# A decoder layer on one core: the first norm's weights spread by a product with ones, and the first block's units begin with the rounded part

## The reference

```
xn   = x * rsqrt(mean(x*x) + 1e-6) * norm_attn      # per row; norm_attn has 1024 values
proj = xn @ w_in                                    # w_in is 1024 x 6664
```

## Time and profile before

| | |
|---|---|
| median of 3 runs | 1675.35 us (1675.06 to 1676.15) |
| the profiled execution | 1674.95 us, its span 1673.2 us |
| TensorE busy | 1649.5 us, 99% of the span |
| VectorE, ScalarE, POOL busy | 951.2, 633.0, 354.0 us |
| granted TensorE clock, mean | 0.997 of full speed |

### The profile page before, as it was taken

One profiled execution on the slowest core, in us unless ns is written; L12 is line 12 of the kernel. 1 busy time (PEld: TensorE's weight loads), 2 busy tenths in 40 slices (PEclk: granted clock), 3 DMA queues, 4 the chain that ended last, 5 costly groups with the idle time before them and its releaser, 6 DMA issues.

```text
span 1673.2 us, 26883 instructions
## 1 busy us (share of the span) xinstructions
PE 1649.5 (99%) x10087; PEld 1494.9 (89%) x10087; DVE 951.2 (57%) x1745; ACT 633.0 (38%) x1403; POOL 354.0 (21%) x353
## 2 busy tenths in 40 slices
PE   8999999999999999999999999999999999999997
PEld 8999999899998899888978899999999999999995
DVE  5413333443145545674544877777777777766787
ACT  5423334232235423553402444333444443344332
POOL 3002001010002200121000233333333222223354
PEclk9999999999999999999999999999999999999999
DMA  7104354562311132311231111111111111110112
GB/s 218 52 28 134 62 74 86 61 88 30 68 29 26 33 77 45 61 26 26 63 132 51 32 45 51 50 50 50 50 29 46 50 50 50 50 46 30 50 63 107
DMA packets 138714, 99.21 MB, mean 59 GB/s; under 512 B 82360, under 2 KB 128448, under 8 KB 138632
## 3 DMA queue, kind: packets, MB, share of 16 engines
q1 hardware_dynamic: 138632, 98.08, 24.2%
HBM read 88.43 MB, written 11.60 MB: 60 GB/s over the span
## 4 chain that ended last, share of the span: by engine, by line
PE 96%; DVE 2%; issue 1%; DMA 1%; ACT 1%; POOL 0%; SPq 0%; DVEq 0%; POOLq 0%; ACTq 0%
PE bank L887 37%; PE bank L1235 23%; PE bank L1215 6%; PE bank L1268 6%; PE bank L1269 6%; PE bank L1267 6%; PE bank L843 3%; PE bank L1276 2%; PE bank L1072 2%; PE bank L1042 1%; PE bank L952 1%; PE bank L944 1%; PE bank L947 1%; PE bank L989 1%; PE bank L927 0%
## 5 line engine op out<-in xcount | busy, mean ns | idle before, releaser
L1235 PE MATMUL bank<-xT_hi,w_hi 128*128 128x384 f32 (+1 forms) x768 | 250.7, 326 | 1.0 <-DVE xT_lo L1819 1.0
L1235 PE MATMUL bank<-xT_hi,w_lo 128*128 128x384 f32 (+1 forms) x768 | 250.6, 326 | 0.0
L1235 PE MATMUL bank<-xT_lo,w_hi 128*128 128x384 f32 (+1 forms) x768 | 250.5, 326 | 0.0
L887 PE MATMUL bank<-xT_hi,w_hi 128*128 128x384 f32 (+1 forms) x1008 | 195.4, 335 | 0.0
L887 PE MATMUL bank<-xT_hi,w_lo 128*128 128x384 f32 (+1 forms) x1008 | 186.3, 326 | 0.0
L887 PE MATMUL bank<-xT_lo,w_hi 128*128 128x384 f32 (+1 forms) x1008 | 186.1, 326 | 0.0
L2495 POOL TENSOR_TENSOR e<-gain_b,e 128x512 f32<-128x512 f32 x60 | 78.0, 1301 | 435.2 <-ACT gain_b L1748 435.2
L887 PEld LDWEIGHTS bank<-xT_lo,w_hi 128*128 128x128 f32 x1008 | 168.7, 188 | 0.0
L887 PEld LDWEIGHTS bank<-xT_hi,w_lo 128*128 128x128 f32 x1008 | 168.7, 188 | 0.0
L887 PEld LDWEIGHTS bank<-xT_hi,w_hi 128*128 128x128 f32 x1008 | 166.1, 188 | 2.7 <-issue 1.0
L1794 DVE TENSOR_TENSOR w_lo<-raw,w_hi 128x1024 fp32r<-128x1024 f32 (+1 forms) x54 | 70.4, 1303 | 158.6 <-ACT w_hi L1387 158.4
(11 more groups left out here) (261 smaller groups left out, 3025.5 us busy)
## 6 DMA issues: line engine op xcount, KB each, us to landing
raw<-in_w_in SPq DMA_DIRECT2D x64, 256.0 KB, 4.6
raw<-in_w_up SPq DMA_DIRECT2D x16, 1024.0 KB, 5.4
raw<-in_w_down SPq DMA_DIRECT2D x16, 1024.0 KB, 5.0
raw<-in_w_in SPq DMA_DIRECT2D x9, 1024.0 KB, 6.3
xin<-in_x_prompt SPq DMA_DIRECT2D x8, 512.0 KB, 4.0
bc<-gate_rows SPq DMA_DIRECT2D x32, 128.0 KB, 7.2
Cin<-in_state_C SPq DMA_DIRECT2D x4, 1024.0 KB, 7.6
out<-Cin SPq DMA_DIRECT2D x16, 256.0 KB, 9.4
```

The lines of the kernel that those rows point to most:

```text
L887: last = nc.tensor.matmul(out, lhsT, rhs, start=(step == 0), stop=(step == 3 * KT - 1))
L1235: last = nc.tensor.matmul(bank[unit_bank(g, u)][:, 0:cn], w[:, 0, k * WCOLS + tile * P:k * WCOLS + (tile + 1) * P], x[:, k, c0:c0 + cn], s ...
```

## The change

`norm_attn` is no longer loaded 128 times over. It comes as one row of 1024 values (4 KB) into the second buffer of `xn`, as the first transfer of all, ahead of x tile 0. POOL writes a row of 128 ones into the first buffer of `xn`. TensorE multiplies ones and row (inner dimension 1) into banks 0 and 1, 512 columns each, and ScalarE copies both banks into `gain_b` before it squares tile 0. VectorE waits for these copies instead of for the load.

The identity products, 14 in one run before, become 6 ahead of the row's products, 6 behind them and 5 behind the transposes of tile 0.

The units of block 0 wait for the rounded halves of their x tile (`norm_hi`) at their start, and for the remainders (`norm_lo`) only ahead of the second pass, which is the first that reads them.

```diff
--- before.py
+++ after.py
@@ -101,7 +101,7 @@
 B_MLP = len(BLOCKS)
 RING = 3
 SPLIT_AT = 3
-WARM = 14
+WARM = 6
 NB = SEQ // P
 MASKW = WIN + (2 * NSEQ - 1) * DSEQ
 UP_UNITS = 2 * len(CHUNKS)
@@ -403,6 +403,8 @@
         w_hi_half = sem("w_hi_half")
         w_lo_done = sem("w_lo_done")
         gain_in = sem("gain_in")
+        gain_mm = sem("gain_mm")
+        gain_cp = sem("gain_cp")
         const_in = sem("const_in")
         consts = sem("consts")
         norm_sq = sem("norm_sq")
@@ -511,6 +513,8 @@
         out_dma = sem("out_dma")
 
 
+        one_row, gain_row = xn[0:1, 0, 0:P], xn[0:1, 1, :]
+
         def w_view(t, b, k):
 
             n = WCOLS + 8 if b == 0 else WCOLS
@@ -633,8 +637,8 @@
                     sp.wait_ge(norm_xn, i - 2)
                 sp.dma_start(xin[0:rows_of(i), i % 3, :], x_rows(i)).then_inc(x_in[i % 3], 16)
 
+            sp.dma_start(gain_row, norm_attn[0].unsqueeze(0)).then_inc(gain_in, 16)
             load_x(0)
-            sp.dma_start(gain_b[:, :], norm_attn[0].partition_broadcast(P)).then_inc(gain_in, 16)
             load_block(0)
             load_x(2)
             small(bias_i[:, :], b_gate[0, 0:MH].unsqueeze(1))
@@ -869,6 +873,8 @@
                     pe.wait_ge(w_hi_done, b + 1)
                 for step in range(3 * KT):
                     (w, x), k = PASSES[step // KT], step % KT
+                    if b == 0 and step == KT:
+                        pe.wait_ge(norm_lo, 2 * (u + 1))
                     if n == 0 and step == KT // 2:
                         pe.wait_ge(w_hi_done, 1)
                     if n == 0 and step == 2 * KT:
@@ -1179,11 +1185,20 @@
                     proj_unit(b, u)
 
             pe.wait_ge(consts, 1)
-            for x in range(WARM):
-                nc.tensor.matmul(bank[3][:, 0:P], ident[:, :], ident[:, :], start=True, stop=True)
+            def identity_products(n):
+                for x in range(n):
+                    nc.tensor.matmul(bank[3][:, 0:P], ident[:, :], ident[:, :], start=True, stop=True)
+
+            identity_products(WARM)
+            pe.wait_ge(gain_in, 16)
+            for h in range(2):
+                nc.tensor.matmul(bank[h][:, :], one_row, gain_row[:, h * 512:(h + 1) * 512],
+                                 start=True, stop=True).then_inc(gain_mm, 1)
+            identity_products(6)
             norm_transposes(0, xn)
+            identity_products(5)
             for u in range(NT):
-                pe.wait_ge(norm_lo, 2 * (u + 1))
+                pe.wait_ge(norm_hi, 2 * (u + 1))
                 proj_unit(0, u)
                 if u + 2 < NT:
                     norm_transposes(u + 2, xn)
@@ -1642,6 +1657,9 @@
                 act.wait_ge(x_in[i % 3], 16 * (i // 3 + 1))
                 square(i, xin[0:rows_of(i), i % 3, :], junk)
 
+            for h in range(2):
+                act.wait_ge(gain_mm, h + 1)
+                nc.scalar.activation(gain_b[:, h * 512:(h + 1) * 512], bank[h][:, :], ACT.Copy).then_inc(gain_cp, 1)
             square_x(0)
             act.wait_ge(raw_first, 32)
             nc.scalar.activation(w_hi[:, 0, part_cols(0, 0)], raw[:, 0, part_cols(0, 0)], ACT.Copy).then_inc(w_first, 1)
@@ -2106,7 +2124,7 @@
                     nc.vector.scalar_tensor_tensor(h, a, 0.5, h, ALU.mult, ALU.add).then_inc(sg_use, 1)
 
 
-            dve.wait_ge(gain_in, 16)
+            dve.wait_ge(gain_cp, 2)
             norm_tile(0, xin[:, 0, :], xn)
             dve.wait_ge(w_first, 1)
             at = part_cols(0, 0)
@@ -2371,6 +2389,7 @@
                                                channel_multiplier=ch)
 
             nc.gpsimd.memset(neghalf[:, :], -0.5)
+            nc.gpsimd.memset(one_row, 1.0)
             link(nc.gpsimd.memset(ident[:, :], 0.0))
             keep_where(ident[:, :], [[-1, P]], 0, 1, ALU.not_equal, 1.0).then_inc(consts, 1)
```

## The result

The changed kernel takes 1679.03 us (median of 14 runs, 1676.52 to 1679.55), the kernel before, on the same chips, 1675.28 us (14 runs). The ratio is 1.0018, its 95% interval 1.0012 to 1.0025: **slower**, by 3.75 us by the medians and by 2.0 to 4.2 us by the interval. I had forecast 1.5, and the time lies outside my range. The ratio is still just inside the 0.2% that I had called "within"; the medians, 0.22% apart, are not. Twelve of the fourteen runs lie between 1678.96 and 1679.55 us; the other two are 1676.52 and 1677.29.

What follows compares the result with a forecast made beforehand. TensorE, busy 99% of the span, was taken as the bound, so only its start could move: second unit at 19.5 instead of 18.05, +1.5 us with POOL's memset, giving 1676.8 us; range 1675.4 to 1678.1.

Steps and rivals of the forecast that it cites:

- within: Whole kernel: time changes by no more than about 0.2% (3.35 us); chance 0.95.
- part 1 and 2: At the start: gain as a row delays tile 0's square to 6.85 us; norms then put the second unit at 19.5.
- The path: Start: row products and copies delay the first square, then xn of tile 2, moving the second unit from 18.05 to 19.5.
- the price of the row's products: TensorE before the first norm: four fp32 instructions of 512 columns, 0.45 us apart at most, the last 0.59 long.
- at the same place as before: TensorE's start: clock falls only behind tile 0's transposes, which with the first rounding run 10.39 to 12.1 us.
- clock falls in the pause: Rival: TensorE idles 7.5 to 10.4 us, transposes of tile 0 run 0.21 apart; +2.35, 1677.7 us; chance 0.12.
- Held steps: Before xn of tile 2: VectorE's remainder holds POOL's first step until 16.6 us; the second takes 0.55, done at 17.2.
- late row: Rival: row lands 4.9 us after issue, row products start at 5.7 us; +2.85, 1678.2 us; chance 0.06.
- The weights of the first half block: Load at the start: weights land about 1.3 us earlier, near 7.0, but nothing waits for them alone any more.
- Part 3: First block's units begin with the rounded part: first unit waits for roundings at 12.1 us; later units gain nothing.
- The five late identity products: TensorE behind tile 0's transposes: start at 11.26, end near 13.4 us; no cost while xn of tile 2 is later.

Runs made afterwards that it cites:

- experiment 9: The changed kernel run again unaltered: 1678.23 us, second unit at 20.32 us.
- Experiment 3: The changed kernel without the row: gain loaded 128 times over again, no row products or copies; 1674.77 us, second unit at 17.75 us.
- experiment 5: The changed kernel with the square of x tile 0 moved ahead of the two gain copies on ScalarE: 1675.62 us against 1675.54 for the kernel before.
- experiment 4: The changed kernel with 14 instead of 6 identity products ahead of the row's products: 1680.57 us, second unit at 22.78 us.
- experiment 1: The kernel before, with only the first block's units beginning with the rounded part: 1675.16 us against 1675.38, ratio 0.9997.
- 8: The changed kernel without the row, with all 14 identity products ahead of the transposes and five behind: 1675.22 us against 1675.54 for the kernel before.
- experiment 11: The changed kernel without the row, gain loaded 128 times over, measured again: 1674.71 us against 1675.14 for the kernel before, ratio 0.9997.
- experiment 6: The changed kernel without the five identity products behind the transposes of tile 0: 1678.80 us, second unit at 22.87 us.
- 7: The changed kernel with twelve instead of six identity products behind the row's products: 1678.68 us, second unit at 21.93 us.
- 10: The changed kernel run unaltered for a second further look: 1678.96 us, second unit at 22.10 us.
- experiment 2: The changed kernel with row products over 128 rows, the tile zeroed first by VectorE and x tile 0 issued before the row: 1678.04 us, ratio 1.0014.
- experiment 12: The changed kernel with row products over 128 rows and the square of x tile 0 ahead of the gain copies: 1675.19 us against 1675.14, ratio 1.0003.

## Why the prediction was wrong

The steps of part 1 and 2, as forecast, in the first profile and in experiment 9 (start in us):

| step | before | forecast | after | exp. 9 |
|---|---|---|---|---|
| second gain copy | | 6.35 | 8.41 | 6.62 |
| square of tile 0 | 4.76 | 6.85 | 8.91 | 7.11 |
| xn of tile 0 | 6.94 | 9.05 | 11.08 | 9.29 |
| transposes of tile 0 | 8.28 | 10.39 | 12.42 | 10.63 |
| square of tile 1 | 10.25 | 12.0 | 14.92 | 13.13 |
| square of tile 2 | 12.53 | 14.0 | 16.93 | 15.14 |
| xn of tile 2 | 15.52 | 17.25 | 19.91 | 18.12 |
| unit 1 | 18.05 | 19.5 | 22.10 | 20.32 |

**The path was right**: the row's products and copies stand ahead of the first square, the chain of norms runs late, xn of tile 2 holds unit 1, and in the first profile the shift reaches the end one to one. Experiment 3 shows that the row is the cause, experiment 5 that ScalarE's order is part of it.

**The term that failed is the price of the row's products**: "so 0.45 apart at most". The fold's row is right for the upper level, and experiments 4 and 9 measured 1.98 us for the four; but I had read the upper level into the start of this kernel, and added only "a little for the slow clock". At the lower level the four took 3.78 us (0.85 apart, 1.02 for the first). Of the 2.06 us by which the square of tile 0 is later than forecast, about 1.4 are the spacing, 0.5 the longer last product and 0.2 to 0.3 the start of the row's products at 4.60 instead of 4.33: POOL's memset of the ones pushed the identity products from 1.61 to 1.74, where I had said some hundredths, and the rest is a gap at the change of operands.

**Where the error came from.** The price needed the upper level to be there when the row's products begin, at 4.6 us. In the kernel before it came up at 4.55, and that was the one profile I had. By the spacing of the starts on TensorE's timeline it came up at:

| what TensorE does from 1.6 or 1.7 us on | level up at (us) |
|---|---|
| 24 or 28 identity instructions without a break (before, experiments 1, 3, 4, 8, 11) | 4.55, 5.8, 5.2, 6.0, 5.3, 5.0 |
| 12 of them, then the products of one row (the first profile, experiments 5, 6, 7, 9, 10) | 17.5, 14.2, 20.6, 12.6, 4.6, 16.0 |
| 12 of them, then the products over 128 rows (experiments 2, 12) | 6.9, 8.0 |

The profile that I had was the earliest of its group. With any of the other five the forecast's price would not have held in full, whatever the one-row products do.

**The same error again at the transposes**: I let the clock fall behind them ("at the same place as before") and gave them 0.64 us to the first rounding. They ran 0.22 apart and moved the square of tile 1 by another 0.86. Going the other way, xn of tile 2 followed its square after 2.98 us and not 3.25. That leaves 2.06 + 0.86 - 0.27 = 2.65 us over the forecast at xn, and 2.6 at the mark.

**The rival "clock falls in the pause"** had the right engine and one of the two places. Its time came true in experiment 9 (20.32 for 20.4), its reason did not: there, as in experiment 4, the level fell behind the row's products while TensorE was busy, and in experiment 2 it held through a pause of 2.7 us. That the number fits is in part luck. The commoner course, in which the upper level isn't reached at all before the row's products, I had not among the rivals; my range ended at 1678.1, and its sum (19.5 + 2.6 at the mark) would have given 1679.4.

**Held steps.** The POOL step did get held by VectorE's remainder, but it was the second one: 1.45 us instead of 0.55, and the first slipped through in 0.19.

```profile
18.15 0.19 POOL L2400 TENSOR_SCALAR rstd<-stat 128x1 f32<-128x1 f32 x1 [1.18 <-ACT junk L1409]
18.21 1.25 DVE L2136 TENSOR_TENSOR w_lo<-raw,w_hi 128x1056 fp32r<-128x1056 f32 x1
...
18.43 1.45 POOL L2402 TENSOR_TENSOR rstd<-rstd,neghalf 128x1 f32<-128x1 f32 x1
```

It started at 18.43 and ended at 19.88, 0.4 us after VectorE's instruction ended at 19.46: the wait, and then most of its own time. The Trainium skill (SBUF — State Buffer, Who interferes with whom) says that the two engines share one pair of ports, that a VectorE instruction with both inputs in SBUF holds it, against a GpSimd instruction that reads SBUF, and that the loser waits for the whole instruction. This trace agrees for the second step, as the earlier trace rows did for the first.

**What else held.** The row's landing is seen nowhere, but no profile with the row first in the queue shows a wait for it, so the rival "late row" did not come. The weights of the first half block landed at 7.5 (2.08 + 5.4 us), 0.8 us sooner than before, where I had estimated 1.3 (7.0), and nothing waited for them alone. x tile 0 landed at 5.2. Part 3 was worth nothing (experiment 1). The five late identity products cost nothing on the path (experiment 6). The formula for the gap in the Trainium skill (TensorE: Matmul & The Clock Gate, Back-to-back issue gap), an estimated 0.22 us at 512 columns, is met by none of the fp32 products here, which are two instructions each: 0.43 for one instruction at the upper level, 0.85 at the lower. The rounded products of 512 columns beside the fold in the kernel before are near it, 0.23 to 0.24 apart.

**What stays open.** In seven profiles with products of one row, the upper level came only behind them in five and was lost behind them in two; with products of 128 rows (experiments 2 and 12) it came among the row's products and stayed. Whether the one row is the reason, or when in an execution the kernel happens to start, nine profiles don't settle, and experiment 2 changed the order of the loads and VectorE's first work as well. The medians of experiments 5 and 12 are lower than their profiles explain, and no profile caught one of their shorter executions. Nor did one catch the changed kernel's 1676.52: by the sum of experiment 5 it needs a mark near 19.6, which is what I had forecast (an estimate).

## What to carry to other kernels

Work that replaces a transfer must be priced at the place where it will stand: at the start of this kernel TensorE's products ran at half the pace that the same shape shows later, in most of the profiles, and the profile's clock column did not say so, only the spacing did. A moment read from one profile, as the 4.55 us at which the level came up, is one draw of several. Before moving work ahead of a chain, look in each engine's list for what stands behind it without needing it (here the square behind the gain copies: one moved line gave 1.45 us at the mark and 3.4 us in the median). And a transfer that is late is worth at most what the next latecomer leaves: in experiment 11, which has the late weights, the second unit waits 0.77 us for xn of tile 2 and not for weights. How much of that wait weights 0.8 us sooner (7.5 for 8.28) would take away without the row, no run shows.

## What the runs showed that I had not expected

- The upper level can be lost behind busy work: in experiment 4 TensorE was busy from 1.74 us on without a pause of note, at the upper level for the row's products (1.98 us for four), and PEclk fell to 0.50 behind them, near 9.4 us, during the identity products.
- One kernel has more than one course at its start: three profiles of the changed kernel gave unit 1 at 22.10, 22.10 and 20.32, with times of 1678.97, 1678.96 and 1678.23. The last came 1.8 us sooner to the mark and only 0.7 to the end.
- The missing microsecond lies at a later wait. From the mark to the end of the span it is 1655.1 to 1655.3 us in eight of the fourteen profiles, but 1656.2 in experiment 9, 1656.4 and 1656.1 in 8 and 12, and 1658.3 and 1658.7 in 2 and 5 (experiment 4 has 1655.8, not followed up). In those five TensorE waits longer for VectorE's step on `Cin` near 188 us: 0.84 us in experiment 12, 1.11 in 8, 1.40 in 9, 1.85 in 2 and 2.36 in 5, where the kernel before and the first profile wait 0.38. That is the whole loss in 9, and half or more of it in 8 and 12. In 2 and 5 the level then falls to 0.50 (near 191.2 and 191.7 us), which costs the 24 products behind the wait another 1.5 us. TensorE's timeline in the kernel before, then in experiment 5:

```profile
185.95 0.41 PE L843 MATMUL bank<-ident,hT 128*128 128x128 f32 x2 [0.38 <-DVE Cin L1910]
```

```profile
190.53 0.41 PE L847 MATMUL bank<-ident,hT 128*128 128x128 f32 x2 [2.36 <-DVE Cin L1928]
...
192.53 1.91 PE L893 MATMUL bank<-w_hi,xT_lo 128*128 128x256 f32 x8
```

So the shift at the mark reaches the end one to one only where this wait stays as it was. Why `Cin` comes later in some executions is not shown.
